# Seven recurrence levels as products of two 64-row groups instead of fourteen zero-padded products

## The reference

```python
cond -> m = cond @ w_mod + b_mod, split in 6 (shift, scale, gate of each half)
h = modulate(rmsnorm(x, norm1_g), sh1, sc1)
aq, ak, av, hq, hzf, hzb, hi, hgate, gu, gv = jnp.split(h @ w_in_l, splits, axis=-1)
att = dense_attention / neighbourhood_attention      # 8 heads of 64
rec, sf, sb = hgrn2_mixer(...)                       # 4 heads of 64, both directions
mlp = chunk_mlp(gu, gv, ...)                         # 4 groups
x = x + g1 * (jnp.concatenate([att, rec, mlp], axis=-1) @ w_out_l)
x = x + g2 * routed_moe(modulate(rmsnorm(x, norm2_g), sh2, sc2), ...)   # 32 experts, top 4
```

```python
a[t, s] = sum_k q[t, k] * key[s, k] * exp(b[t, k] - b[s, k])    # b: running sum of log f
o[t]    = sum_s a[t, s] * v[s]      # the two directions are added
```

## Time and profile before

| | us |
|---|---|
| Median of 3 runs | 1203.01 (1202.03 to 1203.14) |
| The profiled execution | 1201.17 |
| Its span in the trace | 1199.3 |
| PE busy | 1104.8 (92%) |
| DVE busy | 237.1 (20%) |
| ACT busy | 164.3 (14%) |
| PE matmul records / DVE / ACT / POOL | 5486 / 472 / 289 / 39 |

### The profile page before, as it was taken

One profiled execution on the slowest core, in us unless ns is written; L12 is line 12 of the kernel. 1 busy time (PEld: TensorE's weight loads), 2 busy tenths in 40 slices (PEclk: granted clock), 3 DMA queues, 4 the chain that ended last, 5 costly groups with the idle time before them and its releaser, 6 DMA issues.

```text
span 1199.3 us, 14044 instructions
## 1 busy us (share of the span) xinstructions
PE 1104.8 (92%) x5486; PEld 479.1 (40%) x5486; DVE 237.1 (20%) x472; ACT 164.3 (14%) x289; POOL 19.9 (2%) x39
## 2 busy tenths in 40 slices
PE   6899999999999989898989898989898989898985
PEld 2688955544343423242323242323242323242322
DVE  2335761520101111111111111111111111111112
ACT  1222340211010101010101010101010101010102
POOL 0400000000000000000000000000000000000000
PEclk9899999999999999999999999999999999999998
DMA  9995378579999999999999999999999999999992
GB/s 321 336 360 219 114 256 323 211 292 422 422 422 422 422 422 421 422 421 422 421 422 422 422 422 422 422 422 422 422 422 422 422 422 422 422 422 422 422 422 99
DMA packets 79881, 455.36 MB, mean 380 GB/s; under 512 B 7983, under 2 KB 21315, under 8 KB 30582
## 3 DMA queue, kind: packets, MB, share of 16 engines
q1 hardware_dynamic: 76784, 446.73, 91.6%
q0 software_dynamic: 2080, 6.98, 1.7%
q10 hardware_dynamic: 998, 1.39, 0.5%
HBM read 453.36 MB, written 1.70 MB: 379 GB/s over the span
## 4 chain that ended last, share of the span: by engine, by line
DMA 56%; PE 25%; DVE 2%; SPq 2%; issue 1%; ACT 1%; DVEq 0%
DMA ring<-in_w_up 56%; PE bank L1465 16%; PE bank L1335 2%; SPq L366 2%; PE bank L1427 2%; PE bank L1476 1%; PE bank L1133 1%; PE bank L1450 1%; ACT k_pool L631 0%; PE bank L1140 0%; PE bank L1405 0%; PE bank L1369 0%; DVE xres L941 0%; DVE xres L1092 0%; ACT colsT L617 0%
## 5 line engine op out<-in xcount | busy, mean ns | idle before, releaser
L1465 PE MATMUL bank<-ring,colsT 128*64 128x512 f32 x2048 | 466.7, 598 | 47.1 <-DMA ring<-in_w_up 32.9
L1465 PEld LDWEIGHTS bank<-ring,colsT 128*64 128x64 f32 x2048 | 136.5, 137 | 373.4 <-issue 226.8
L1465 PE MATMUL bank<-ring,k_pool 128*64 128x512 f32 x1024 | 226.8, 595 | 14.9 <-ACT k_pool L631 14.9
L1465 PEld LDWEIGHTS bank<-ring,k_pool 128*64 128x64 f32 x1024 | 70.7, 137 | 149.7 <-issue 127.9
L1014 DVE TENSOR_SCALAR k_pool<-bank 128x512 f32<-128x512 f32 x32 | 22.1, 692 | 539.7 <-PE bank L1465 539.7
L1427 PEld LDWEIGHTS bank<-keyT,rows 128*128 128x128 f32 x544 | 66.7, 196 | 26.2 <-issue 25.1
L1427 PE MATMUL bank<-keyT,rows 128*128 128x128 f32 x544 | 73.2, 288 | 0.3 <-ACT colsT L617 0.3
L1018 DVE TENSOR_SCALAR k_pool<-bank 128x512 f32<-128x512 f32 x32 | 22.1, 691 | 233.9 <-PE bank L1465 233.9
L1476 PE MATMUL bank<-d_pool,colsT 64*128 64x512 f32 x264 | 65.6, 615 | 0.0
L627 ACT ACTIVATE k_pool<-k_pool 128x512 f32<-128x512 f32 x32 | 20.2, 630 | 243.9 <-DVE k_pool L1014 243.9
L1181 PE MATMUL bank<-colsT,ring 128*128 128x256 f32 x224 | 49.6, 380 | 1.1 <-DVE colsT L729 0.8
(11 more groups left out here) (295 smaller groups left out, 531.4 us busy)
## 6 DMA issues: line engine op xcount, KB each, us to landing
ring<-in_w_gate SPq DMA_DIRECT2D x128, 1024.0 KB, 24.4
ring<-in_w_up SPq DMA_DIRECT2D x128, 1024.0 KB, 26.3
ring<-in_w_down SPq DMA_DIRECT2D x128, 1024.0 KB, 24.4
ring<-in_w_mod SPq DMA_DIRECT2D x24, 1024.0 KB, 11.3
ring<-in_w_in SPq DMA_DIRECT2D x13, 1024.0 KB, 12.7
ring<-in_w_out SPq DMA_DIRECT2D x4, 1024.0 KB, 6.3
k_pool<-in_const_masks POOLq DMA_DIRECT2D x1, 1024.0 KB, 8.0
g<-in_b_mod POOLq DMA_DIRECT2D x2, 512.0 KB, 11.6
```

The costliest lines, as they stand in the source:

```text
L1465: ins = mm(bank[CAP * half:CAP * (half + 1), :], lhsT(2 * r + kk), w[:, kk, 512 * half:512 * (half + 1)], start=m == 2 and r == 0 and kk = ...
```

## The change

- A level is now one product for both directions: `Kl[:, n % 2]` holds forward keys in the first halves and backward keys in the second halves, `Ql[:, n % 2]` the queries the other way round. Neither has zeros, and every place is written at every level.
- Head q is contracted over its own 64 partitions and goes to bank 2 + q: eight products of 64x128 by 64x128 per level in place of two times four of 128x128.
- `level_store` copies 512 columns of each bank under a mask of the level that takes both directions. The masks come as bytes (128 KB) straight into `masks`; the cast and the two clearings by GpSimd go, with their waits.
- Keys and queries have two buffers, taken in turn by n.
- Order on PE: the diagonal moves ahead of `Q_0`, level n stands behind the projection with index n from `Q_0` on (Q_0, K_1, Q_1, V_0, V_1, G_V, G_U), and none is left with `H_G`. ACT's exponentials and DVE's steps move with them; the store of level 6 moves between the evictions of the attention and the gating.

```diff
-    m = np.zeros((P, 16, P), np.float32)
+    m = np.zeros((P, 8, P), np.uint8)
     for n, w in enumerate(LEVELS):
-        same = s // (2 * w) == t // (2 * w)
-        first, second = s % (2 * w) < w, t % (2 * w) >= w
-        m[:, n] = same & first & second
-        m[:, 7 + n] = m[:, n].T
-    m[:, M_DIAG] = s == t
+        m[:, n] = (s // (2 * w) == t // (2 * w)) & (s // w != t // w)
...
-        Kl = k_pool[:, 0:1024].rearrange("p (d n) -> p d n", d=2)
-        Qpair = gain.rearrange("p (d a q n) -> p d a q n", d=2, a=4, q=2)
+        Kl = k_pool[:, 0:1024].rearrange("p (o n) -> p o n", o=2)
+        Ql = gain.rearrange("p (o n) -> p o n", o=2)
...
-            small_load("masks_loaded", k_pool, const_masks)
+            small_load("masks_loaded", masks.rearrange("p m t -> p (m t)"), const_masks)
...
-            pool.wait_ge(ev("masks_ready"), 1)
-            nc.gpsimd.memset(Kl, 0.0).then_inc(ev("k_zero"), 1)
             pool.wait_ge(ev("h_ready"), 4)
-            nc.gpsimd.memset(gain, 0.0).then_inc(ev("k_zero"), 1)
...
             copy_win(K_0)
+            level_exp(0)
             copy_win(Q_0)
-            level_exp(0)
+            level_exp(1)
...
-            level_exp(3)
+            level_exp(4)
             copy_win(V_1)
-            level_exp(4)
+            level_exp(5)
...
-            level_exp(5)
             level_exp(6)
...
-            dve.wait_ge(ev("masks_loaded"), 16)
-            V.tensor_copy(masks.rearrange("p m t -> p (m t)"), k_pool).then_inc(ev("masks_ready"), 1)
...
-            def level_qk(n, d):
+            def level_qk(n):
                 w = LEVELS[n]
-                dve.wait_ge(ev("lvl_exp"), 4 * n + 2 * d + 2)
-                dve.wait_ge(ev("lvl_mm"), max(1, 2 * n + d))
-                if n == 0:
-                    dve.wait_ge(ev("k_zero"), 2)
-                ex_ = level_view(Dl[:, d, :], w)
-                for q in range(2):
-                    hd = slice(HD * q, HD * (q + 1))
-                    V.tensor_tensor(Qpair[hd, d, :, q, :].rearrange("p a (n m) -> p a n m", m=w),
-                                    ...
-                V.tensor_tensor(level_view(Kl[:, d, :], w)[:, :, d, :], ex_[:, :, d, :],
-                                level_view(keyT[:, d, :], w)[:, :, d, :], ALU.mult).then_inc(ev("lvl_qk"), 1)
+                K, Q = level_view(Kl[:, n % 2], w), level_view(Ql[:, n % 2], w)
+                dve.wait_ge(ev("lvl_exp"), 4 * n + 4)
+                if n != 1:
+                    dve.wait_ge(ev("lvl_mm"), max(1, n))
+                for d in range(2):
+                    x = level_view(Dl[:, d, :], w)
+                    V.tensor_tensor(Q[:, :, 1 - d, :], x[:, :, 1 - d, :], level_view(hqT, w)[:, :, 1 - d, :], ALU.mult).then_inc(ev("lvl_qk"), 1)
+                    V.tensor_tensor(K[:, :, d, :], x[:, :, d, :], level_view(keyT[:, d, :], w)[:, :, d, :], ALU.mult).then_inc(ev("lvl_qk"), 1)
...
-            def level_store(n, d):
+            def level_store(n):
...
-                    V.copy_predicated(AT[:, q, :].rearrange("p (a n h m) -> p a n h m", a=4, h=2, m=w)[:, :, :, 1 - d, :],
-                                      ...
+                    V.copy_predicated(AT[:, q, :].rearrange("p (a t) -> p a t", a=4),
+                                      masks[:, n, :].unsqueeze(1).to_broadcast([P, 4, P]),
+                                      B[2 + q].rearrange("p (a t) -> p a t", a=4)).then_inc(ev("lvl_store"), 1)
...
-            def level(n, d):
-                pe.wait_ge(ev("lvl_qk"), 6 * n + 3 * d + 3)
-                pe.wait_ge(ev("lvl_store"), max(2, 4 * n + 2 * d))
+            def level(n):
+                pe.wait_ge(ev("lvl_qk"), 4 * n + 4)
+                pe.wait_ge(ev("lvl_store"), 2 * n + 2)
                 for m in range(4):
-                    ins = mm(B[2 + d][:, P * m:P * (m + 1)], Kl[:, d, P * m:P * (m + 1)], Qpair[:, d, m],
-                             start=True, stop=True)
+                    for q in range(2):
+                        hd = slice(HD * q, HD * (q + 1))
+                        ins = mm(B[2 + q][:, P * m:P * (m + 1)], Kl[hd, n % 2, P * m:P * (m + 1)],
+                                 Ql[hd, n % 2, P * m:P * (m + 1)], start=True, stop=True)
...
-            pe.wait_ge(ev("lvl_store"), 30)
+            pe.wait_ge(ev("lvl_store"), 2 * len(LEVELS) + 2)
```

More of the change, by code:

```diff
@@ L1263, in _ @@
                 ins.then_inc(ev("pT_ps"), 1)
-            project_with_levels(G_U, 5)
+            project_with_level(G_U, 6)
             pe.wait_ge(ev("pT_ready"), 2)
@@ L1277, in _ @@
             ins.then_inc(ev("z_ps"), 1)
-            project(H_G, between=lambda: level(5, 1))
-            level(6, 0)
+            project(H_G)
             pe.wait_ge(ev("gmlp_ready"), 1)
             scores(4, 1, lambda hd, h: kT[hd, h, 1, :])
-            level(6, 1)
             scores(6, 1, lambda hd, h: ckT[hd, h, :]).then_inc(ev("score_s"), 1)
```

82 lines of the change are left out of this document (35 added, 47 removed).

## The result

The change made the kernel faster, by more than was forecast. The median is 1191.68 us (1191.23 to 1194.54, 4 runs) against 1203.08 (1202.03 to 1204.49, 4 runs): ratio 0.9912, interval 0.9898 to 0.9926, 11.4 us.

A forecast was written before the change was run, and what follows sets the result against it. Bound by the expert weight stream, which starts when PE reaches the experts. Gains 3.8 - 0.55 + 1.6 + 1.7 + 0.28 = 6.8 us take the median 1203.01 to 1196.2 us, range 1193.7 to 1200.2.

The forecast's parts named there:

- What bounds the kernel: Whole kernel: the expert weight stream starts when PE reaches the experts, so the end moves one for one with PE's arrival.
- Levels, 3.8: PE's seven levels: 12.66 us before, 8.86 after with 64-row products and changes of row form; gain 3.8 us.
- The rival of row groups wholly side by side (0.45): Levels: both row groups fully parallel, 0.45 + 0.2 us a level, gain 4.5 more, time 1191.7; chance 0.04.
- Level 4's wait, 0.55: Behind the scores and V_1: PE waits for all four exponentials and four DVE products; loss 0.55 us, bounds 0 and 1.5.
- The mixer's end, 1.6: Behind the second scores: PE's waits for Kend, Qend and level 6's store go, only the transposes stay; gain 1.6 us.
- The clock, 1.7: mod_sums(4) behind the mixer: without PE's 1.41 us idle the clock no longer falls; gain 1.7 us.
- 0.9 MB less is moved ... gain 0.28, at most: At 32 to 40 us: lighter masks remove PE's only DMA wait there, for the weights of H_Q; gain at most 0.28 us.
- that offset: Whole kernel: the profiled execution of before lay 1.8 us below its median, so forecast 1194.4 became 1196.2 against the median.
- The range: Whole kernel: 1193.7 (better ends of all terms but a group's price, spread 1.1) to 1200.2 (clock and a new wait).

The follow-up runs named there:

- e12_order_bytes: Kernel before with the new order and byte masks, but the old zero-padded products, buffers and clearings: 1197.13 us, ratio 0.9945.
- e2_new_order: Kernel before with only the order of the kernel after; zero-padded products, float32 masks and buffers kept: 1199.42 us, ratio 0.9974.
- e11_bytes_traffic: Kernel before with byte masks plus an unused 1 MB load where the float32 masks were, GpSimd's clearing of the keys waiting for it: 1200.90 us, ratio 0.9986.
- e10_bytes_again: Kernel before with only byte masks loaded straight into place, no cast, run again in another batch: 1198.43 us, ratio 0.9957.
- e1_byte_masks: Kernel before with only byte masks loaded straight into place, no cast, clearings kept: 1198.25 us, ratio 0.9963.
- e14_masks_last: Kernel before with float32 masks, cast and clearings kept, but the masks' load moved behind POOL's other early loads: 1198.40 us, ratio 0.9964.
- e3_new_form: Kernel after's 64-row products, byte masks and two buffers, in the order of the kernel before: 1194.95 us, ratio 0.9936.

## Why the prediction was wrong, and where it was right

- **What bounds the kernel: right.** The end moved with PE's arrival at the experts. Levels 5.8 us sooner gave the whole 5.8 at the end, and the stretch behind `mod_sums(4)` is 1033.4 us in both; over all traces it is 1033.1 to 1034.9.
- **Levels, 3.8: right within 0.2.** From `e12_order_bytes` to the kernel after is 3.81 us of trace, with level 4's wait of 0.17 in it, so 3.98 without. The two row groups run at 1.09 to 1.10 us for eight products, as the scores and the diagonal did, and a change between 128-row and 64-row work costs what was read off. The rival of row groups wholly side by side (0.45) is refuted.
- **Level 4's wait, 0.55: too large.** From `V_1` to the level PE takes 119.61 - 112.34 = 7.27 us where others have 7.10: 0.17. DVE's timeline shows why:

```profile
118.13 0.42 DVE L784 TENSOR_TENSOR gain<-d_pool,hq_hi 128x256 f32<-128x256 f32 x1 [2.94 <-ACT d_pool L512]
118.47 0.42 DVE L785 TENSOR_TENSOR k_pool<-d_pool,keyT 128x256 f32<-128x256 f32 x1
118.81 0.42 DVE L784 TENSOR_TENSOR gain<-d_pool,hq_hi 128x256 f32<-128x256 f32 x1
119.14 0.42 DVE L785 TENSOR_TENSOR k_pool<-d_pool,keyT 128x256 f32<-128x256 f32 x1
```

Four products run at 0.34 us from start to start, and only the last has its whole 0.42. The prediction multiplied the length of one by four, 1.75 us; they took 1.43. This is an error of reading: a row's length holds the overlap with the next.
- **The mixer's end, 1.6: right in size.** The order in the old form gives 1.67. With the clock, `e2_new_order` has 3.2 us for the 3.3 forecast. It is not a gain of the order alone: the new form would have brought most of it in the old order too.
- **The clock, 1.7: right in the two profiled executions** (1.80 with the rest of that stretch). Over the five traces that fell its mean is 2.3 us, since the fall is sometimes twice as long; the profiled one had the short fall. But byte masks alone keep the clock in the old order too, so behind them order and clock bring 1.3 us in the medians, 2.0 less than the forecast.
- **"0.9 MB less is moved ... gain 0.28, at most": this step failed.** Byte masks alone gave 4.4 and 4.5 us. The 0.28 was the idle entry of PE's wait for `H_Q` in one trace, taken as the bound of what the traffic could cost. From start to start that wait cost 29.38 - 28.85 = 0.53 even there, and 1.07, 0.87 and 0 in other traces of before, a mean of 0.62. By the experiments the 4.5 are 2.5 of traffic (`e11_bytes_traffic` against `e10_bytes_again`) and 2.0 that stay gained with the traffic back in place. For these the traces offer two terms: in the old order and form the clock holds where it fell (2.3), and DVE's wait is 0.35 shorter. Of the 2.5 the traces place only the 0.6 before `H_Q`; the mean clock of the runs suggests up to 1.7 more, at a place that no trace shows. In the kernel after, whose clock holds at the mixer's end anyway, putting the traffic back costs 1.6 to 3.0.
- **The start of the kernel was not in the sum at all.** It has 1.6 us of the difference of the two profiled executions. By the means of the traces (41.2 us in four of before, 40.1 in two of after) it is 1.1, and it is all in the clock. PE's work up to there is the same in both kernels, and `e1_byte_masks`, with light traffic, has its first projection at 42.4. So nothing shows that the change caused it, and luck of the profiled executions is the simpler account.
- **The profiled execution and the median.** Before's lay 1.8 us below its median, and the forecast carried that offset over. After's lies at its median (1191.45 and 1191.68). The kernel before has more that differs from run to run (two falls of the clock and the wait for `H_Q`), and the profile had caught a good run.
- **The range.** Only level 4's wait had a better end, 0.55, and with the spread of 1.1 the lower bound would be 1194.5. The 0.8 us down to 1193.7 have no working.

The miss of 4.5 us in steps. Between the profiled executions it is 9.8 - 6.8 = 3.0: start 1.6, the wait for `H_Q` 0.25, DVE's wait 0.35, level 4 0.4, the levels, the clock and the rest 0.4. The offset to the median is the other 1.6, to within 0.1. In the medians of the one batch with all steps it is another sum: 4.2 from the masks, 1.6 from the form, less 2.0 for order and clock, 3.8 in all. So part of the masks' error is hidden by what they took from the clock's term. The forecast terms of the levels and the mixer's end held in their mechanism. What was missing was the price of a load that nothing visibly waited for.

What stays open is how the masks' traffic costs about 2 us per MB in the medians and only 0.6 in the traces' waits. In all, the means of the traces, four of before and two of after, give 1.1 + 0.6 + 5.8 + 2.1, and 0.35 behind `mod_sums(4)`: 10.0 us, as their spans do. The medians differ by 11.4 in one batch and 10.7 in the other; so 0.7 to 1.4 us lie in runs of which there is no trace. Open too is why DVE's wait is 0.35 us shorter in four kernels.

## What to carry to other kernels

A wait in one profiled execution is no upper bound for what a load costs: where the wait is small and the stage's times scatter from run to run, price the load by its bytes at the stage's bandwidth (here 2.5 us per MB against 1.6 to 3.0 measured), and look whether it can go later; `e14_masks_last` got the whole gain by moving the load and its cast behind the other early loads. Look at several executions before a term is taken from a clock fall or an early wait, and take repeated instructions from start to start, not by their length. Two parts of a change that remove the same idle time, or the same fall of the clock, must be counted once. Compare kernels whose runs were taken together: here before's own median moved by 1.4 us from batch to batch, as much as some of the effects.

## What was not expected of the hardware

- The clock falls in a stretch with little idle. PE idled 1.41 us before the fall of before, 0.48 before that of `e3_new_form`, and 1.05 to 1.11 in four kernels without one. A fall at the mixer's end costs 1.7 or 3.2 us.
- One unused product of 512 columns (1.12 us in the trace) at each of two waits, with later bias loads, kept the clock at 1.00 through the kernel's start in the profiled execution, and took the scatter of six runs from 5.8 us to 0.5. Three at each, 2.84 us, kept the clock too and cost what that saved.
- Eight float32 products over 64 rows in two row groups took 1.09 us, four over 128 rows 0.89: by the estimate of 1.78 one after the other and 0.45 wholly side by side, the two groups overlap, but far from wholly.
